# Exponentials behind the next half split, and a pooling stage by pairs of blocks, in a two-block transformer kernel on one Trainium2 core

## The reference

```python
def second_block(x, rel_bias, ln_g, ln_b, ffn_w_gu, ffn_w_down, a_w_in, a_w_out, ...):
    for i in range(DEPTH_2):
        x = layer_norm(DEEPNORM_ALPHA * x + 0.5 * swiglu(x, ffn_w_gu[i, 0], ffn_w_down[i, 0]), ...)
        if kind == 0:
            y = moba_attention(x, a_w_in[j], a_w_out[j], rel_bias)
        elif kind == 1:
            y = pool_mixer(x, b_w_in[j], b_w_group[j], b_scale[j], b_w_out[j])
...
        x = layer_norm(DEEPNORM_ALPHA * x + y, ln_g[i, 1], ln_b[i, 1])
        x = layer_norm(DEEPNORM_ALPHA * x + 0.5 * swiglu(x, ffn_w_gu[i, 1], ffn_w_down[i, 1]), ...)
    return x
```

## Time and profile before

| | |
|---|---|
| median of 3 runs | 1638.83 us |
| lowest, highest | 1637.58, 1642.01 us |
| the profiled execution | 1638.96 us |
| its span in the trace | 1637.2 us |
| mean granted TensorE clock | 0.982 of full |
| busy: VectorE, ScalarE, GpSimd | 998.6, 773.7, 162.4 us |

### The profile page before, as it was taken

One profiled execution on the slowest core, in us unless ns is written; L12 is line 12 of the kernel. 1 busy time (PEld: TensorE's weight loads), 2 busy tenths in 40 slices (PEclk: granted clock), 3 DMA queues, 4 the chain that ended last, 5 costly groups with the idle time before them and its releaser, 6 DMA issues.

```text
span 1637.2 us, 30488 instructions
## 1 busy us (share of the span) xinstructions
PE 1588.5 (97%) x12680; PEld 1540.2 (94%) x12680; DVE 998.6 (61%) x1281; ACT 773.7 (47%) x1017; POOL 162.4 (10%) x132
## 2 busy tenths in 40 slices
PE   7999999988999999999999899999999999899997
PEld 5999998877999999999999789999999999899997
DVE  5876895344776645655466666554665557775545
ACT  3544555443455534544444455444544445554433
POOL 0100002333200001000012002000210013020001
PEclk9999999989999999999999999999999999999999
DMA  8974763222545555455545324555355554345550
GB/s 318 366 264 155 293 230 125 101 78 96 184 148 189 185 190 191 156 181 185 191 162 181 129 103 180 179 183 191 141 205 179 180 182 153 135 175 183 185 194 30
DMA packets 42154, 289.68 MB, mean 177 GB/s; under 512 B 4843, under 2 KB 7019, under 8 KB 7500
## 3 DMA queue, kind: packets, MB, share of 16 engines
q1 hardware_dynamic: 41244, 284.44, 47.8%
q0 software_dynamic: 816, 3.87, 0.6%
HBM read 285.15 MB, written 3.15 MB: 176 GB/s over the span
## 4 chain that ended last, share of the span: by engine, by line
PE 88%; DVE 6%; ACT 3%; issue 2%; DMA 1%; POOL 0%; SPq 0%; ACTq 0%; DVEq 0%; POOLq 0%
PE banks L612 21%; PE banks L615 21%; PE banks L614 21%; PE banks L713 6%; PE banks L715 6%; PE banks L716 6%; DVE w_lo L1599 2%; ACT w_hi L1160 1%; DVE XS L1747 1%; PE banks L958 0%; PE banks L744 0%; PE banks L869 0%; DMA raw<-in_panels 0%; PE banks L961 0%; DVE H L1755 0%
## 5 line engine op out<-in xcount | busy, mean ns | idle before, releaser
L1599 DVE TENSOR_TENSOR w_lo<-raw,w_hi 128x1024 fp32r<-128x1024 f32 x490 | 612.6, 1259 | 510.8 <-ACT w_hi L1160 505.5
L1160 ACT ACTIVATE w_hi<-raw 128x1024 fp32r<-128x1024 f32 x490 | 515.0, 1057 | 560.9 <-PE banks L615 408.3
L612 PE MATMUL banks<-H,w_lo 128*128 128x256 f32 x1920 | 541.8, 282 | 2.2 <-DVE H L1755 1.6
L614 PE MATMUL banks<-H,w_hi 128*128 128x256 f32 x1920 | 540.2, 281 | 0.0
L615 PE MATMUL banks<-H,w_hi 128*128 128x256 f32 x1920 | 540.2, 281 | 0.0
L612 PEld LDWEIGHTS banks<-H,w_lo 128*128 128x128 f32 x1920 | 361.3, 188 | 5.3 <-issue 3.4
L614 PEld LDWEIGHTS banks<-H,w_hi 128*128 128x128 f32 x1920 | 361.4, 188 | 0.0
L615 PEld LDWEIGHTS banks<-H,w_hi 128*128 128x128 f32 x1920 | 361.4, 188 | 0.0
L614 PE MATMUL banks<-HH,w_hi 128*128 128x256 f32 x960 | 270.1, 281 | 0.0
L612 PE MATMUL banks<-HH,w_lo 128*128 128x256 f32 x960 | 270.1, 281 | 0.0
L615 PE MATMUL banks<-HH,w_hi 128*128 128x256 f32 x960 | 270.1, 281 | 0.0
(11 more groups left out here) (285 smaller groups left out, 1716.9 us busy)
## 6 DMA issues: line engine op xcount, KB each, us to landing
raw<-in_panels SPq DMA_DIRECT2D x269, 1024.0 KB, 4.8
bias_rows<-rev POOLq DMA_DIRECT2D x1, 2048.0 KB, 16.9
XS<-in_x_t SPq DMA_DIRECT2D x1, 1024.0 KB, 6.5
near<-bias_rows POOLq DMA_DIRECT2D x8, 128.0 KB, 3.0
out_t<-XS SPq DMA_DIRECT2D x4, 256.0 KB, 2.6
ws<-in_ws_t POOLq DMA_DIRECT2D x1, 512.0 KB, 9.3
cols<-in_cols SPq DMA_DIRECT2D x1, 180.0 KB, 2.4
wdt<-in_wdt POOLq DMA_DIRECT2D x1, 128.0 KB, 5.7
```

Of the source, the lines that this page charges most:

```text
L612: pe.matmul(acc, w_lo[:, panel_slot, at:at + P], operand[:, kk, 0, :], start=starts and c == chunks[0], stop=False)
L614: pe.matmul(acc, w_hi[:, panel_slot, at:at + P], operand[:, kk, 1, :], start=False, stop=False)
L1160: act.activation(w_hi[:, sl, w], raw[:, r, w], ACT.Copy).then_inc(panel_hi, 1)
L1599: vec.tensor_tensor(w_lo[:, sl, w], raw[:, r, w], w_hi[:, sl, w], ALU.subtract).then_inc(panel_lo, 1)
```

## The change

In the attention ScalarE's step i now begins with the split. Behind it come the exponentials of the heads scored in step i - 1, then, in steps 3 and 7, the copies of the values, then the turned probabilities and the rounding. The copies of the values lose their own wait, since the split in front of them waits for the same half.

In the pooling the second panel of pool_in's second group is multiplied block by block in the order 2, 3, 0, 1. A new semaphore `pool_block` tells when blocks 2 and 3 are done; ScalarE copies them out (`pool_pair_kept(1)`, with a new semaphore `pool_kept`), and blocks 0 and 1 at the end. Sums, means, rounding and remainder of these four blocks go by the two pairs, and so do TensorE's group products, which wait for the first pair and then for the second. The order of the splits in between moves on both engines.

```diff
+POOL_BLOCKS = (2, 3, 0, 1)
...
                     pe.wait_ge(panel_lo, 2 * q + 1)
-                    for b in range(BANKS):
+                    for b in blocks:
                         for c in range(4):
-                            if b == 0 and c == 2:
+                            if b == blocks[0] and c == 2:
                                 pe.wait_ge(panel_lo, 2 * q + 2)
                             last = product(b, c)
-                            if b == BANKS - 1 and c % 2:
+                            if b == blocks[-1] and c % 2:
                                 last.then_inc(half_used, 1)
                             elif c == 3:
                                 last.then_inc(each, 1)
...
+                        if name == "pool_in" and g == 1 and p == 1:
+                            products((FIRST_GROUP[s] + u) % 2, FIRST_PANEL[s] + 3, split_slot(s, u, p), operand, 4, False, True,
+                                     each=S["pool_block"], blocks=POOL_BLOCKS)
+                            continue
...
-                for b in range(BANKS):
+                for b in POOL_BLOCKS if n else range(BANKS):
                     m = BANKS * (1 - n) + b
+                    if n and b == 0:
+                        pe.wait_ge(S["pool_lo"], 3)
...
             for i in range(14):
+                q, half = att_half(i)
+                split(q + SPLIT, *raw_place(q + SPLIT), halves=(half,))
+                for h in HEADS_SCORED.get(i - 1, ()):
+                    exps(h)
                 if i in (3, 7):
-                    act.wait_ge(half_used, 2 * FIRST_PANEL[INDEX["vals"]] + i + 1)
                     for t in range(TT):
                         act.activation(v_tok[:, t, i // 4 * CHUNK:i // 4 * CHUNK + CHUNK], banks[:, value_bank(i // 4, t), :],
                                        ACT.Copy).then_inc(S["v_copied"], 1)
-                q, half = att_half(i)
-                split(q + SPLIT, *raw_place(q + SPLIT), halves=(half,))
                 for h in HEADS_TURNED.get(i, ()):
                     probs_turned(h)
                 for h in HEADS_SUMMED.get(i, ()):
                     head_rounded(h)
-                for h in HEADS_SCORED.get(i, ()):
-                    exps(h)
...
+            def pool_pair_kept(w):
+
+                s = INDEX["pool_in"]
+                if w:
+                    act.wait_ge(S["pool_block"], 2)
+                else:
+                    products_done(s, 1)
+                bank = BANKS * ((FIRST_GROUP[s] + 1) % 2) + 2 * w
+                act.activation(pu[:, 2 * w:2 * w + 2, PAD:], banks[:, bank:bank + 2, 0:T], ACT.Copy)\
+                    .then_inc(S["pool_kept"] if w else taken, 1)
...
             split_ahead(4)
+            pool_pair_kept(1)
             pool_rounded(0)
+            pool_pair_kept(0)
             split_ahead(5, (0,))
-            pool_kept(1)
+            pool_rounded(1)
+            pool_rounded(2)
+            pool_scaled(0)
             split_ahead(5, (1,))
-            pool_scaled(0)
-            pool_rounded(1)
             split_ahead(6, (0,))
...
             pool_rest(0)
+            vec.wait_ge(S["pool_kept"], 1)
+            doubled(0, 2, 4)
+            doubled(1, 2, 4)
+            pool_means(1)
             split_ahead(4, (1,))
             vec.wait_ge(taken, FIRST_GROUP[INDEX["pool_in"]] + 2)
-            doubled(0, 0)
-            doubled(0, 1)
-            pool_means(1)
+            pool_rest(1)
+            doubled(0, 0, 2)
+            pool_means(0)
+            pool_rest(2)
             split_ahead(5, (0,))
-            pool_rest(1)
             pool_scaled(0)
```

More of the change, by code:

```diff
@@ L301, in two_blocks @@
             "pt_done pt_copied o_done o_hi o_lo "
-            "pool_hi pool_lo pool_f pads_clear pool_y_hi pool_y_lo inv_loaded x_stored").split()}
+            "pool_hi pool_lo pool_f pads_clear pool_block pool_kept pool_y_hi pool_y_lo inv_loaded x_stored").split()}
         block = ctx.enter_context(nc.Block())
@@ L603, in _, with products @@
         def _(pe):
-            def products(group_u, q, panel_slot, operand, k, starts, stops, chunks=range(4), ready=None, each=None):
+            def products(group_u, q, panel_slot, operand, k, starts, stops, chunks=range(4), ready=None, each=None,
+                         blocks=range(BANKS)):
                 def product(b, c):
@@ L1540, in split_ahead, with pool_kept @@
                 split(q, *raw_place(q), halves=halves)
-            def pool_kept(n):
-                s, g = INDEX["pool_in"], 1 - n
-                products_done(s, n)
-                act.activation(pu[:, BANKS * g:BANKS * g + BANKS, PAD:], group_banks((FIRST_GROUP[s] + n) % 2), ACT.Copy)\
-                    .then_inc(taken, 1)
+            def pool_kept():
+                s = INDEX["pool_in"]
+                products_done(s, 0)
+                act.activation(pu[:, BANKS:KD, PAD:], group_banks(FIRST_GROUP[s] % 2), ACT.Copy).then_inc(taken, 1)
+            def pool_pair_kept(w):
+                s = INDEX["pool_in"]
+                if w:
[5 more added lines that the diff above has]
+                    .then_inc(S["pool_kept"] if w else taken, 1)
             def pool_rounded(n):
-                b = slice(BANKS * (1 - n), BANKS * (2 - n))
+                b = (slice(BANKS, KD), slice(2, 4), slice(0, 2))[n]
                 act.wait_ge(S["pool_f"], n + 1)
@@ L2138, in split_ahead, with doubled @@
                 split(q, *raw_place(q), halves=halves)
-            def doubled(g, w):
-                first, last = max(2 * w, BANKS * g), BANKS * g + BANKS
+            def doubled(w, first, last):
                 reach = 2 ** w
@@ L2149, in doubled, with pool_means @@
                 step(vec.tensor_tensor(here[:, :, PAD:], there[:, :, PAD:], there[:, :, PAD - reach:PAD + T - reach], ALU.add))
-            def pool_means(n):
-                g, edge = 1 - n, max(WINDOWS)
+            def pool_means(*pairs):
+                edge = max(WINDOWS)
                 vec.wait_ge(S["inv_loaded"], 16)
-                for w in (2 * g, 2 * g + 1):
+                for w in pairs:
                     b, sums = slice(2 * w, 2 * w + 2), pw[:, LEVEL[w]:LEVEL[w] + 2, PAD:]
@@ L2180, in _ @@
             vec.wait_ge(S["pads_clear"], 2)
-            doubled(1, 0)
-            doubled(1, 1)
+            doubled(0, BANKS, KD)
+            doubled(1, BANKS, KD)
             split_ahead(3, (1,))
-            doubled(1, 2)
-            doubled(1, 3)
-            pool_means(0)
+            doubled(2, BANKS, KD)
+            doubled(3, 6, KD)
+            pool_means(2, 3)
             split_ahead(4, (0,))
             pool_rest(0)
+            vec.wait_ge(S["pool_kept"], 1)
+            doubled(0, 2, 4)
+            doubled(1, 2, 4)
+            pool_means(1)
             split_ahead(4, (1,))
             vec.wait_ge(taken, FIRST_GROUP[INDEX["pool_in"]] + 2)
-            doubled(0, 0)
-            doubled(0, 1)
-            pool_means(1)
+            pool_rest(1)
+            doubled(0, 0, 2)
+            pool_means(0)
+            pool_rest(2)
             split_ahead(5, (0,))
-            pool_rest(1)
             pool_scaled(0)
```

4 lines of the change are left out of this document (2 added, 2 removed).

## The result

| | before | after |
|---|---|---|
| median, in runs side by side | 1639.57 us (4 runs, 1637.58 to 1642.01) | 1624.25 us (4 runs, 1623.43 to 1628.89) |
| the profiled execution | 1638.96 us | 1624.63 us |
| its span | 1637.2 us | 1622.9 us |
| mean granted TensorE clock | 0.982 | 0.985 |

The ratio is 0.9912, with an interval of 0.9888 to 0.9935: faster by 0.9%.

The account below looks back on a forecast made before the run. The prediction took TensorE, busy 97% of the span, as the bound. From 1638.96 us it took 7.6 (attention) and 3.7 (pooling), giving 1627.7, less 0.1 to the median: 1627.6 us, range 1625.5 to 1632.5.

Parts of the forecast that it names:

- part 1: Attention: ScalarE's new order, split before exponentials, removes nearly all of nine TensorE waits; 7.6 us gained.
- part 2: Pooling: two waits of 1.2 and 1.5 us replace one of 4.1 us, clock stays up; 3.7 us gained.
- another 1.6 us: Allowance in the range, should borders elsewhere in the kernel keep their clock better at their new times.
- the step of 4.42 us: Attention: TensorE's unhindered time for one step, against 5.27 us in the kernel before.
- the 0.2 us from start to start: Attention: each of nine waits costs 0.2 us beyond its listed idle time, measured between matmul starts.
- head 0's wait: Attention: the one wait for normalized probabilities expected to remain, about 0.3 us in the profile after.
- 0.55 of room: Attention: the low part is done at 4.85 us, 0.55 us before the next step's value products need it.
- The first rival: Pooling: the clock falls all the same in the two shorter waits, costing 2.1 us; 1629.7 us, chance 0.27.
- The low part becomes the ring: Attention: VectorE delivers the low part late, about 3.5 us of the gain kept back; 1631.1 us, chance 0.10.
- the third rival: Attention: the next split is held up by copies, so only the pooling counts; 1635.1 us, chance 0.05.
- The attention only changes its wait: Attention: copies behind the exponentials hold up ScalarE's next split, only the pooling gains; 1635.1 us, chance 0.05.
- exponentials one step late: Attention: TensorE waits out split, exponentials and normalization, 2.8 us for each of eight heads; about 1649 us, chance 0.03.

Follow-up runs that it names:

- The kernel before with filler: The kernel before, with 30 matmuls into an unused bank during TensorE's long pooling wait; 1636.64 us, ratio 0.9984.
- wait by banks: The changed kernel, with pool_out's first group waiting for each of its four banks apart instead of all four; 1629.41 us, ratio 0.9939.
- the exponentials put last: The changed kernel, with ScalarE's exponentials moved behind the turned probabilities and the head's rounding, to the step's end; 1631.78 us, ratio 0.9956.
- the attention alone: The kernel before, with only ScalarE's new order in the attention loop; 1628.98 us, ratio 0.9953.
- pooling alone: The kernel before, with everything of the change except ScalarE's attention loop; 1635.79 us, ratio 0.9989.
- after again: The changed kernel measured a second time with no edit; 1628.46 us, ratio 0.9943.
- both wait by banks and filler: The changed kernel with pool_out waiting for each bank apart, plus 20 matmuls in TensorE's output-stage wait for `MX`; 1627.14 us, ratio 0.9924.

## Why the prediction was wrong, point by point

**The sum has no term for the 900 us ahead of the attention: the step that failed.** "1638.96 - 7.6 - 3.7 = 1627.7" takes everything ahead of the first wait that goes as coming again to the tenth of a microsecond. Between the two profiles this part, put at nothing, was worth 4.2 us, the largest error of the sum: 4.2 + 0.1 (part 1) - 1.2 (part 2) - 0.1 (behind the pooling) makes the 3.0 us that are missing between 11.3 and 14.3. The same instructions end there anywhere in 9 us in ten profiles, for the most part by where the clock falls in the first 480 us. The range held only "another 1.6 us" for this, and called it borders keeping their clock better at new times, as if the change did it. By the scatter of the table it needed about 4 us on either side of an 11 us gain, an estimate.

That the number came out too low and not too high is for the larger part chance: three of after's first four runs, from 1623.43 to 1624.63 us, lie below all six later ones. Those six gave 1628.46 us, close above the forecast of 1627.6 and inside its range, and there the medians are 10.2 us apart and the ratio says 9.3, beside 7.7 + 2.5 = 10.2 of the two stages. The median of all ten is 1627.0. Even so the 1627.6 is near it partly by luck, since part 2 was forecast 1.2 us too high.

**Part 1, 7.6 us gained: right.** 7.7 in the stage, and 7.7 by the ratio of the run of it alone. The pieces held too: the step of 4.42 us to the hundredth, the 0.2 us from start to start for each wait beside its idle time (idle time alone, 6.3 - 0.3, would have fallen short by 1.7 us), head 0's wait at 0.26 us where "about 0.3" was said. The low part ended 0.46 to 0.52 us before its use, where 0.55 of room was laid out.

**Part 2, 3.7 us gained: mechanism right, one term missed.** The first remainder was to release TensorE at 1397.55 and the second at 1400.5. After's axis lies 11.91 us earlier (first group product against first group product); its 1385.66 and 1388.58 are 1397.57 and 1400.49 on before's. Wrong was "VectorE has split its first half by 1401.5 and the first scaled block by 1401.9, and each further block follows in 0.41 us against 1.4 us of matmuls". That takes the operand for the only thing pool_out waits for. It also takes over four banks that VectorE is still reading, and one wait (`psum_free`) stands for all four: VectorE's fourth block ended at 1391.23, on before's axis 1403.14, and pool_out began at 1403.20 and not at 1402.0. In the earlier trace rows this isn't to be seen as a wait, because there the banks were free in time. VectorE scaled the four blocks of before right behind the second remainder:

```profile
1400.37 1.65 DVE L2173 SCALAR_TENSOR_TENSOR H<-banks,cols,H 128x256 fp32r<-128x256 f32 x4
```

It was through at 1402.02, while 24 matmuls still stood between that remainder and pool_out. At 0.12 us each they would have lasted until about 1403.5, so the lowered clock isn't what hid the wait. The kernel before with filler shows it at a clock of 1.00: VectorE is through at 1404.67, and pool_out follows the last group product of 1405.99 without a wait.

```profile
1403.02 1.65 DVE L2175 SCALAR_TENSOR_TENSOR H<-banks,cols,H 128x256 fp32r<-128x256 f32 x4
```

```profile
1406.11 0.28 PE L612 MATMUL banks<-H,w_lo 128*128 128x256 f32 x1
```

The wait is the change's own work, then: only 12 matmuls, 1.4 us, follow the second remainder now, and VectorE's split of pool_out's first half, 1.22 us, now stands between that remainder and the scaled blocks, where it stood ahead of the remainder. The run with the wait by banks got back 1.08 us of the 1.2, and with it the stage is 3.60 us shorter than in before, against 3.7 forecast. Of these 2.2 us are the clock (2.1 forecast), by the run with filler in the kernel before.

**The clock at 1.00 in the pooling: right.** The first rival (chance 0.27) asked for 0.50 behind the second wait; all six profiles with the split wait have 1.00 from 1365 to 1425 us, with idle times of 1.1 and 1.3 us, and in four of them 1.0 us more, within 7 us. The reason given, that no wait of the attention brought the clock down, holds too: it is 1.00 from 895 to 960 us in all ten. The Trainium skill (TensorE: Matmul & The Clock Gate, A second HAM failure mode: psum-queue depth-cycling) tells of a kernel whose frequent short idle times between groups of matmuls made the clock go down again and again; these two or three in a row did not.

**The other rivals.** *The low part becomes the ring* didn't happen in after; with the exponentials put last it did in part, at 2.4 us for the stage against the 3.5 us given. The range said that it took in "the third rival" but ended at 1632.5, below that one's 1635.1; it took in the low part's 1631.1. *The attention only changes its wait* and *exponentials one step late* fell with the first run of the attention alone: 7.7 us came. The single wait of 0.26 us, head 0's, says that they are late nowhere else.

**What stays open.** Why the clock falls at one wait in one execution and not in the next. The Trainium skill (TensorE: Matmul & The Clock Gate, What's actually happening) calls the start of the chip's watching free of the kernel's start, so that the same kernel is caught differently from run to run; the two executions around 392 us fit that, and no run here tests it. It puts the cost of the slow matmuls at a kernel's start below 1% of a typical span and advises against fitting their count. Here the falls lie in the middle of the kernel; 9 us of 1638 is 0.5% as well, but it is nearly the whole of this change's effect. Open also is a pattern in the table: the attention began at 898.3 to 903.5 us in the six kernels with the new attention and at 903.9 to 907.3 in the four with the old, though no instruction ahead differs. If order were chance, six and four would part so cleanly, this way round, once in 210 times, so ten profiles can't rule out that a part of it is systematic; the 0.7 us between 150 and 250 us may be such a part, but two kernels with the old attention are ahead of before by them as well (pooling alone, and before with matmuls in the wait). Against a large one stand the ratios, each over five runs or more: the new attention alone gained 7.7 us and its stage shows 7.7, after again 9.3 against 10.2, the wait by banks 10.0 against 11.3. Nowhere there is the earlier begin left over. Only the kernel with both wait by banks and filler shows 12.5, of which its own filler explains up to 1.5.

## What to carry to other kernels

Before setting a sum of parts against one profile, add up what the granted clock took in the parts that the edit doesn't touch, and put that spread into the range; compare two versions by stages cut at the same instructions, where 1 us shows, and not by one total each. When a late operand is brought forward, list everything else the waiting instruction needs, bank releases included, and what the new order puts in front of those: a wait for all banks at once became the next bound here the moment the operand was early. When an engine both feeds a bottleneck and works in a ring behind another's output, put the work that waits only for the bottleneck first, and what has a step of room behind it.

## What the runs showed of the hardware that was not expected

- The same instructions ahead of the attention took from 898.3 to 907.3 us in ten profiles. Between 20 and 480 us the granted clock left out 17.0, 20.5, 22.2, 23.9 or 29.0 us of full speed; at the same 22.2 us the attention began from 902.0 to 904.8.
- An identical wait isn't an identical clock: behind the same wait of 2.75 and 2.74 us the granted clock was 1.00 in one execution of the changed kernel and 0.50 in another, which cost it 2.8 us.
- At a granted clock of 1.00, a hundred matmuls of one stage, from 178 us on, started 0.1200 us apart in both profiles of the kernel before and 0.1187 in both of the changed one.
- The one wait of 4.1 us came with a clock of 0.50 in all three profiles that have it unfilled; that of 2.4 to 2.5 us for `MX` in six of nine, at 1.3 to 1.5 us each; those of 1.0 to 1.3 us in the pooling in none of the six that have them.
- 30 filler matmuls in the wait of 4.1 us kept 1.00 and were worth 2.3 us, and no cost of theirs is to be seen: the operand is used 0.44 us after they end.
- Over 24 runs of the kernel before, 0.007 of mean granted clock (0.978 to 0.985) went with 8.7 us of time.
